# Hybrid pooling / short-convolution decoder layer: the third convolution term on ScalarE and GpSimd, more tile buffers, other load conditions and another order

## The chip, the cores and the metric

The program runs on the 8 cores of one Trainium2 chip, each with a different part of the batch and no exchange between them. The metric is the device time of one execution, that of the slowest core, in microseconds. On every core TensorE (PE in the profile), VectorE (DVE), ScalarE (ACT), GpSimd (POOL) and SyncE (SP) each work through an instruction queue of their own in a fixed order. GpSimd and SyncE also issue the transfers.

## What is computed

Each core takes one prompt of 2048 rows and 16 decode sequences of 4 rows (64 rows), all 1024 wide. The reference, cut:

```
h = rmsnorm(x, g_pre_mix) * (1 + sc1) + sh1          # sc1, sh1, gt1, ... = silu(c) @ w_ada + b_ada
v_pool, x_conv, gate_b, gate_c = split(h @ w_in)     # 512 columns each
y_pool = pool_mixer([pool_buf, v_pool]) * pool_scale # windows 2/4/8/16, one 128x128 map per group
y_conv = gate_b * causal_dwconv([conv_buf, gate_c * x_conv], conv_w)   # 3 taps
x = x + gt1 * rmsnorm([y_pool | y_conv] @ w_out, g_post_mix)
h2 = rmsnorm(x, g_pre_ffn) * (1 + sc2) + sh2
a, b = split(causal_dwconv([ffn_buf, h2 @ ffn_w_up], ffn_conv_w))      # 2 x 2816 columns, 3 taps
x = x + gt2 * rmsnorm((silu(a) * b) @ ffn_w_down, g_post_ffn)
```

A `causal_dwconv` with three taps is `p[t-2]*w0 + p[t-1]*w1 + p[t]*w2`. Also returned are the last rows of the pooling input, the convolution input and the up-projection.

## The kernel before

**Stages.** Rows go in tiles of 128: tiles 0 to 15 are the prompt, tile 16 the 64 decode rows. Columns of the transposed activation `ah` go in chunks of 512 rows of the sequence (c = 0 to 3) and chunk 4 for the decode rows.

1. Start: `tile_in(t)` loads a pair of x tiles, ScalarE squares and sums a tile, a square root and a reciprocal follow, VectorE scales it into `xn` (three buffers, which the square also uses as its junk output), TensorE transposes it (8 matmuls against `idb`) and VectorE or ScalarE copies the result to `ah`. Meanwhile GpSimd issues eight `scp` loads, each with one slice of the scale weights and one of the pooling weights. `scale_in(kc)` turns a slice into the factor `g1t`, `start_step(kc, c)` multiplies `ah` by it and adds slice kc to the pooling projection of chunk c, in banks that seven projections hold together.
2. Projections: `pool_one(g, c)` (`P:`), `pool_win(g, c)` (`W:`, windows on VectorE), `conv_mm(j, c)` (24 matmuls into three banks, weights in `ring` buffers), `conv_mid(j, c)`. For a prompt chunk `conv_mid` does: ScalarE x_conv + bias from a bank into `xc`; VectorE `q` = (gate_c + bias) * `xc` from a second bank; ScalarE gate_b + bias from the third bank into `tb`; ScalarE `ta` = w2 * q; VectorE twice `ta` += w * q for the other taps; GpSimd `by` = `ta` * `tb`. `xc`, `q`, `ta` and `tb` have two buffers each, used in turn. There are 16 such prompt units and 4 small ones (chunk 4, 64 elements).
3. `pool_fold` (`F`) multiplies the pooling map into `wo`, the 4 MB of w_out that `wout_load` (`w`) loads into a region where the pooling inputs `v` lay.
4. Output projection: `o_step` runs tile by tile: 16 matmuls `wo,by`; norm on ScalarE; scaling with the gate row `gtp` on VectorE; four additions of 128x256 on GpSimd to x loaded again; store of y; the next norm, and transposes four steps later. `gtp` comes through a scratch tensor in HBM (`gate_scratch`).
5. FFN: `up_group(0)`, down-projection, `up_group(1)`, down-projection, over `w_up` slices in the three `ring` buffers (`up_load`, first three only after `gtp`).

**What sets the order.** The text `PROJ` gives the steps of stages 1 to 3 in TensorE's order (letters as in the table `steps`: `T` tile_in, `a` scale_in, `s` start_step, `m`/`v` the two halves of a conv unit, `U` a whole one, `A` the second set of scale vectors, `w` the w_out load). A planner, `Sched.order`, then plays the whole program with costs (`c_act`, `c_dve`, `c_pool`, `RATE`) and fixes the order of each engine: an instruction's key is the first TensorE step that needs it. Up to a planned time of 70 us a transfer also waits for the last one that had landed in the plan. `keep_warm` puts matmuls on zeros (`ps<-zero`) where the plan sees TensorE wait over 0.5 us. `Region.alias` makes a buffer wait for the last uses of what lay there before.

## Time and profile before

| | us |
|---|---|
| median of three runs | 727.0 (725.28 to 727.85) |
| the profiled execution, its own time | 726.18 |
| its span on core 2, the slowest | 724.6 |
| the spans of the eight cores | 718.5 to 724.6 |
| TensorE busy, core 2 | 694.0 (96%) |
| VectorE / ScalarE / GpSimd busy | 468.5 / 311.1 / 267.5 |

The profiled execution took 1.6 us more than the span of its slowest core and is 0.8 us below the median. The mean granted TensorE clock was 0.989 to 0.995 on the eight cores. The page's picture in 40 slices of 18 us shows TensorE at 9 tenths or more nearly everywhere from the seventh slice on, and 5, 8, 8, 9, 9, 8 tenths in the first six. Busy time of TensorE includes the matmuls on zeros.

### The profile page before, as it was taken

The numbers are of one execution on the slowest core, as the hardware profiler recorded it, in microseconds if no ns is written. First come the engines' busy times: TensorE is split into PE (matmuls) and PEld (weight loads), VectorE is DVE, ScalarE is ACT, GpSimd is POOL, SyncE is SP. The second block draws the span as 40 slices with busy tenths as digits, with TensorE's granted clock in tenths as the row PEclk, the third lists the DMA queues.
The fourth block names the chain that finished last, engine by engine and source line by source line (L and its number), as shares of the span: only waits on it lengthen the run. The fifth ranks groups of instructions, "written<-read, shape, count | busy, mean of one in ns | idle before, by whom it ended". The sixth has DMA issues, their size and how long they took to land.

```text
span 724.6 us, 12059 instructions; the slowest of 8 cores (718.5 to 724.6 us)
## 1 busy us (share of the span) xinstructions
PE 694.0 (96%) x4049; PEld 331.3 (46%) x4049; DVE 468.5 (65%) x636; ACT 311.1 (43%) x554; POOL 267.5 (37%) x274
## 2 busy tenths in 40 slices
PE   5889989999989999999999999999999999999996
PEld 2445535444445544444444444444444444444442
DVE  2659699754659998777777411138777777758403
ACT  5255544334657764444544211144454544433111
POOL 1102255333858634424444132214333333223220
PEclk8999999999999999999999999999999999999999
DMA  8999877996999667556899964113335433061422
GB/s 249 161 240 181 194 124 131 156 192 169 178 277 275 221 116 124 97 127 100 147 156 155 221 222 137 58 59 59 59 66 95 74 59 59 1 228 68 144 105 72
DMA packets 23532, 100.71 MB, mean 139 GB/s; under 512 B 3184, under 2 KB 3696, under 8 KB 18608
## 3 DMA queue, kind: packets, MB, share of 16 engines
q0 software_dynamic: 9072, 47.71, 39.9%
q1 hardware_dynamic: 14400, 52.23, 22.6%
...
HBM read 127.02 MB, written 20.63 MB: 204 GB/s over the span
## 4 chain that ended last, share of the span: by engine, by line
PE 73%; DMA 14%; issue 4%; DVE 4%; POOL 2%; ACT 2%; DVEq 0%; SPq 0%; POOLq 0%; ACTq 0%
PE ps L520 72%; DMA big<-x 5%; DMA scp<-w_scp 3%; DMA y<-big 2%; POOL big L559 2%; DMA wsh<-w_sh 1%; DMA ring<-w_inc 1%; PE ps L530 1%; DVE big L555 1%; POOL by L559 1%; DVE ta L555 1%; DVE ss L559 0%; DVE q L555 0%; PE ps L538 0%; ACT xc L551 0%
## 5 line engine op out<-in xcount | busy, mean ns | idle before, releaser
L520 PE MATMUL ps<-ah,ring 128*128 128x512 bf16 (+2 forms) x2240 | 407.2, 342 | 4.4 <-DVE q L555 2.0
L520 PEld LDWEIGHTS ps<-ah,ring 128*128 128x128 bf16 x2240 | 187.8, 98 | 212.8 <-issue 6.6
L555 DVE SCALAR_TENSOR_TENSOR big<-ps,misc,big 128x1022 f32<-128x1022 f32 (+1 forms) x176 | 224.5, 1281 | 69.5 <-ACT halob L551 32.5
L559 POOL TENSOR_TENSOR g<-big 128x1024 bf16<-128x1024 f32 x44 | 104.5, 2375 | 171.6 <-DVE big L559 91.0
L551 ACT ACTIVATE big<-ps,misc 128x1024 f32<-128x1024 f32 x88 | 97.9, 1113 | 140.1 <-PE ps L520 139.9
L520 PE MATMUL ps<-wdn,g 128*128 128x512 bf16 x704 | 153.1, 379 | 0.0
L559 POOL TENSOR_TENSOR big<-big 128x256 f32<-128x256 f32 (+2 forms) x51 | 65.1, 1279 | 121.0 <-DVE big L555 94.1
L520 PEld LDWEIGHTS ps<-wdn,g 128*128 128x128 bf16 x704 | 68.5, 98 | 82.1 <-issue 0.4
L551 ACT ACTIVATE big<-ps 128x1024 bf16<-128x1024 f32 (+2 forms) x30 | 28.9, 964 | 123.4 <-PE ps L520 116.2
L666 DVE RECIPROCAL stat<-stat 128x1 f32<-128x1 f32 (+1 forms) x64 | 9.7, 157 | 106.3 <-ACT stat L551 105.6
L520 PE MATMUL ps<-wo,by 128*128 128x512 bf16 x256 | 58.2, 384 | 0.0
L551 ACT ACTIVATE big<-big 128x1024 f32<-128x1024 f32 x44 | 46.5, 1057 | 6.5 <-DVE big L555 4.1
L551 ACT ACTIVATE xn<-big 128x1024 bf16<-128x1024 f32 (+1 forms) x27 | 28.4, 1054 | 43.3 <-PE ps L520 17.6
L520 PEld LDWEIGHTS ps<-wo,by 128*128 128x128 bf16 x256 | 24.9, 99 | 28.3 <-issue 1.3
L555 DVE SCALAR_TENSOR_TENSOR big<-ps,stat,gtp 128x1024 f32<-128x1024 f32 x26 | 33.3, 1280 | 2.3 <-DVE stat L666 1.2
L559 POOL TENSOR_TENSOR by<-ta,tb 128x512 bf16<-128x512 f32 x16 | 25.8, 1613 | 24.0 <-DVE ta L555 21.1
L538 PE MATMUL ps<-idb,xn 128*128 128x128 bf16 (+1 forms) x268 | 21.2, 226 | 11.7 <-DVE xn L564 9.8
L555 DVE SCALAR_TENSOR_TENSOR ta<-q,misc,ta 128x512 f32<-128x512 f32 x32 | 24.6, 778 | 5.3 <-ACT ta L551 4.8
L538 PEld LDWEIGHTS ps<-idb,xn 128*128 128x128 bf16 (+1 forms) x268 | 17.7, 102 | 19.9 <-issue 16.1
L564 DVE TENSOR_SCALAR xn<-big,stat 128x1024 bf16<-128x1024 f32 (+1 forms) x27 | 23.0, 859 | 0.5
L570 POOL DMA_DIRECT2D ring<-w_up x22 | 12.8, 583 | 21.9 <-PE ps L520 21.9
L520 PE MATMUL ps<-ah,scp 128*128 128x512 bf16 (+1 forms) x104 | 18.9, 332 | 1.8 <-ACT tb L551 1.0
...
## 6 DMA issues: line engine op xcount, KB each, us to landing
...
wdn<-w_down POOLq DMA_DIRECT2D x11, 512.0 KB, 12.8
wg<-w_gate POOLq DMA_DIRECT2D x4, 1024.0 KB, 11.1
...
```

The source lines that it names most:

```text
L520: inst = e.matmul(bank_ap, l, r, start=(first and i == 0), stop=(last and i == len(pairs) - 1))
L530: inst = e.matmul(o, ls[i], r, start=(i == 0), stop=(i == len(ls) - 1))
L538: inst = e.transpose(o, i, ident)
L551: return K.op("act", lambda e: e.activation(out=out, in_=in_, func=func, **kw), reads=reads, writes=writes, cost=c_act(n, ptr))
L555: return K.op(eng, lambda e: e.scalar_tensor_tensor(out, in0, s, in1, op0, op1), reads=reads, writes=writes, cost=c_dve(n))
L559: return K.op(eng, lambda e: e.tensor_tensor(out, in0, in1, op), reads=reads, writes=writes, cost=c_dve(n) if eng == "dve" else c_pool(n))
L564: return K.op("dve", lambda e: e.tensor_scalar(out, in0, s1, None, op0), reads=reads, writes=writes, cost=c_dve(n, mode), port=mode > 1.0)
L570: return K.dma(eng, lambda e: [e.dma_start(out=dst, in_=src)], sem or next_misc(), 1, reads=reads, writes=regs, deps=deps, nbytes=nbytes)
L666: K.op("dve", lambda e: e.reciprocal(STAT[0:rows, k + 1, t:t + 1], STAT[0:rows, k + 1, t:t + 1]), reads=[r_stat[k + 1][t]], writes=[r_stat ...
```

## The change

- `conv_mid`: tap w0 is no longer added by VectorE. ScalarE writes w0 * q into `xc` (free once q is made), GpSimd adds it to `ta`, VectorE adds tap w1 with its one remaining multiply-add, and VectorE, not GpSimd, multiplies by `tb`. The same for the 4 small units.
- `pool_win` on chunk 4: the 10 running sums over `vs` go from VectorE to GpSimd. The four scalings of the pooling map (`poolw`) and the four 15-column state copies (`npp`) go from VectorE to ScalarE.
- Norms: tiles 0 to 7 have 7 `xn` buffers in place of 3, and the squares of the first norm write to `junk` buffers. The second norm of the prompt tiles writes to 8 `xnp` buffers, which lie where the w_ss weights were.
- A square root without use runs on ScalarE right after the first activation, so that its table is loaded then.
- `wout_load`: the first half of `wo` waits for `v` of groups 0 and 1 only, the second for `v` of groups 1 (second buffer), 2 and 3; before, both waited for all of `v`, `vs` and `pwf`.
- `PROJ` is another text (all tokens of the start are interleaved: chunk 0 is projected before tiles 5 and 7 are turned), and some planner costs are other numbers (`RATE` 315e3 for 330e3; `c_pool`, `c_dve`).
- `turn_by_dma` and `UPAT` are added but not used: with `FIRST_T = 16` every turn stays on TensorE, and with `UPAT = (-1, -1, -1)` the first `w_up` loads wait for the gate row as before.

```diff
 PROJ = """
-T:0 T:1 T:2 T:3 T:4 T:5 T:6 T:7 a:0 s:0,0 s:0,1 a:1 s:1,0 s:1,1 a:2 s:2,0 s:2,1 a:3 s:3,0 s:3,1 a:4 s:4,0 s:4,1
+T:0 T:4 T:1 a:0 T:2 T:3 T:6 a:1 a:2 s:0,0 T:7 T:5 s:1,0 s:0,1 s:2,0 s:1,1 a:3 s:3,0 s:2,1 s:3,1 a:4 a:5 a:6
...
+FIRST_T = 16
+UPAT = (-1, -1, -1)
...
-    RATE = 330e3
+    RATE = 315e3
...
+    K.op("act", lambda e: e.activation(out=STAT[:, 7, 19:20], in_=EPSB, func=AF.Sqrt), reads=[r_sc, r_eps], cost=0.3)
...
+        if k == ST2 and t < 16:
+            N, r_n = XNP[t % 8], r_xnp[t % 8]
+        else:
+            j = t % (NXN + 4) if t < 8 else t % NXN
+            N, r_n = XN[j], r_xn[j]
...
+        if k == ST1:
+            h = t % 2 if t < 8 else 0
+            stats(X[0:rows, :], rows, k, t, [r_x], JUNK[h][0:rows, :], [r_junk[h]])
...
-            ts(POOLW[:, g, :], PWF[:, g, :], VECS[:, V_PSC + g:V_PSC + g + 1], None, ALU.mult, None, [r_pwf, r_vecs], [r_poolw], 128)
+            act(POOLW[:, g, :], PWF[:, g, :], AF.Copy, [r_pwf, r_vecs], [r_poolw], 128, scale=VECS[:, V_PSC + g:V_PSC + g + 1])
...
-                tt(dst[:, lo:W], src[:, lo:W], src[:, lo - sh:W - sh], ALU.add, [r_src], [r_dst], W - lo)
+                tt(dst[:, lo:W], src[:, lo:W], src[:, lo - sh:W - sh], ALU.add, [r_src], [r_dst], W - lo, eng="pool")
...
         act(sh(TA[k]), v[2], AF.Copy, [rq, r_vecs], [r_ta[k]], n, scale=w2)
-        for m, w in ((1, w1), (0, w0)):
-            stt(sh(TA[k]), v[m], w, sh(TA[k]), ALU.mult, ALU.add, [rq, r_ta[k], r_vecs], [r_ta[k]], n)
+        act(sh(XC[k]), v[0], AF.Copy, [rq, r_vecs], [r_xc[k]], n, scale=w0)
+        tt(TA[k][:, 0:n], TA[k][:, 0:n], XC[k][:, 0:n], ALU.add, [r_ta[k], r_xc[k]], [r_ta[k]], n, eng="pool")
+        stt(sh(TA[k]), v[1], w1, sh(TA[k]), ALU.mult, ALU.add, [rq, r_ta[k], r_vecs], [r_ta[k]], n)
         if c < 4:
-            tt(BY[:, 4 + j, c0:c0 + n], TA[k], TB[k], ALU.mult, [r_ta[k], r_tb[k]], [r_by[4 + j][c]], n, eng="pool")
+            tt(BY[:, 4 + j, c0:c0 + n], TA[k], TB[k], ALU.mult, [r_ta[k], r_tb[k]], [r_by[4 + j][c]], n)
...
-            ts(NPP[:, g, :], VB[g][1][:, 528 - PB:528], BIAS[:, g:g + 1], None, ALU.add, None, [r_v[g][1], r_bias], [r_npp], PB)
+            act(NPP[:, g, :], VB[g][1][:, 528 - PB:528], AF.Identity, [r_v[g][1], r_bias], [r_npp], PB, bias=BIAS[:, g:g + 1])
...
             for r in r_wo[hb]:
-                r.alias(pool_regs)
+                r.alias(r_v[0] + r_v[1] if hb == 0 else r_v[1][1:] + r_v[2] + r_v[3])
```

**How the order moves.** TensorE in the start, before: all eight tiles are turned (`idb,xn`), then the slices `scp_59` to `scp_66` are worked off in pairs.

```order
L538 MATMUL ps<-idb_50,xn_96 128x128 x8
L538 MATMUL ps<-idb_50,xn_97 128x128 x8
L513 MATMUL ps<-zero_127 128x512 x12
L538 MATMUL ps<-idb_50,xn_95 128x128 x8
L538 MATMUL ps<-idb_50,xn_96 128x128 x8
L520 MATMUL ps<-sc_45,scp_59 128x18 x8
L520 MATMUL ps<-sc_45,scp_60 128x18 x8
L810 MATMUL ps<-ah_87,scp_59 128x512 x7
```

The same place now:

```order
L519 MATMUL ps<-zero_139 128x512 x17
L544 MATMUL ps<-idb_50,xn_105 128x128 x8
L544 MATMUL ps<-idb_50,xn_119 128x128 x8
L526 MATMUL ps<-sc_45,scp_60 128x18 x8
L837 MATMUL ps<-ah_95,scp_59 128x512 x4
L837 MATMUL ps<-ah_95,scp_60 128x512 x4
L544 MATMUL ps<-idb_50,xn_122 128x128 x8
L526 MATMUL ps<-sc_45,scp_61 128x18 x8
```

Chunk 0's projections (x4) now stand after five tiles; behind the last slice stand 13 matmuls on zeros ahead of tile 8, where none stood, and 6 more ahead of the first use of the second `ring` weights. In all there are 82 such matmuls for 59.

VectorE, first conv units after the decode rows' bias is known, before (with what each waits for):

```order
L555 SCALAR_TENSOR_TENSOR q_99<-raw_89,bias_52,xc_101 128x512 [waits e_pool]
L555 SCALAR_TENSOR_TENSOR by_88<-s_114,v_123 128x512 [waits e_act]
L555 SCALAR_TENSOR_TENSOR by_88<-s_113,v_121 128x512 [waits e_dve]
L564 TENSOR_SCALAR poolw_125<-pwf_126,misc_43 128x128
L555 SCALAR_TENSOR_TENSOR by_88<-s_112,v_118 128x512
L555 SCALAR_TENSOR_TENSOR ta_103<-q_99,misc_43,ta_103 128x512 [waits e_act]
```

And now:

```order
L561 SCALAR_TENSOR_TENSOR ta_111<-q_107,misc_43,ta_111 128x512 [waits e_pool]
L565 TENSOR_TENSOR by_96<-ta_111,tb_113 128x512 [waits e_dve]
L561 SCALAR_TENSOR_TENSOR ta_112<-q_108,misc_43,ta_112 128x512 [waits e_pool]
L561 SCALAR_TENSOR_TENSOR q_107<-ps,bias_52,xc_109 128x512 [waits e_pool,e_pe,e_act]
L565 TENSOR_TENSOR by_96<-ta_112,tb_114 128x512 [waits e_dve]
L561 SCALAR_TENSOR_TENSOR q_108<-ps,bias_52,xc_110 128x512 [waits e_pe,e_pool,e_act]
```

`ta` and `q` now both stand behind waits for GpSimd, and the `poolw` scalings are gone from here.

GpSimd at the end of the projections, before: the first of the three first `w_up` loads (`ring_78`) waits for the gate row, the other two for matmuls that still use their buffers, `ring_77` for those of the last conv unit.

```order
L559 TENSOR_TENSOR by_88<-ta_103,tb_105 128x512
L570 DMA ring_78<-w_up 128x4096
L570 DMA ring_79<-w_up 128x4096
L570 DMA ring_77<-w_up 128x4096
L1015 COPY qlast_108<-q_100 128x2
L559 TENSOR_TENSOR by_88<-ta_104,tb_106 128x512
```

And now:

```order
L565 TENSOR_TENSOR ta_111<-ta_111,xc_109 128x512
L576 DMA ring_86<-w_up 128x4096
L576 DMA ring_85<-w_up 128x4096
L1046 COPY qlast_116<-q_108 128x2
L576 DMA ring_87<-w_up 128x4096
L565 TENSOR_TENSOR ta_112<-ta_112,xc_110 128x512
```

`ring_85`, which waited for the last conv unit, now waits for an earlier one (unit 3 of chunk 3 comes earlier in `PROJ`) and stands ahead of `ring_87`. The gate row's own matmuls (`wg,sc`) come 7.8 us of TensorE work sooner, and SyncE's store of it stands ahead of one store that it stood behind. On the same queue the two `wo` loads stood behind all six w_ss loads and two products; now they directly follow the fifth w_ss load, ahead of the sixth.

## Rows read from the trace of the kernel before

**Rows 1.** Windows, core 2: start:end, length, busy time by engine, clock, DMA share, GB/s
```profile
core 2: us, PE busy (x) PEld busy (x) DVE busy (x) ACT busy (x) POOL busy (x), PEclk, DMA share, GB/s
14.00:52.00 38.00, 31.29 (x242) 17.00 (x243) 22.95 (x57) 14.65 (x37) 5.12 (x11) 0.94 1.03 212
52.00:82.00 30.00, 30.00 (x271) 16.30 (x269) 23.55 (x54) 17.12 (x40) 5.50 (x6) 1.00 1.00 198
82.00:140.00 58.00, 53.04 (x393) 26.16 (x391) 54.61 (x106) 24.07 (x48) 30.00 (x41) 0.97 0.82 138
140.00:176.00 36.00, 35.17 (x206) 16.42 (x205) 18.05 (x30) 14.92 (x23) 9.97 (x15) 1.00 0.87 174
176.00:242.00 66.00, 62.17 (x366) 31.01 (x365) 46.99 (x81) 44.46 (x95) 49.22 (x63) 0.97 0.95 243
242.00:282.00 40.00, 39.00 (x204) 18.51 (x203) 39.13 (x50) 24.64 (x44) 18.93 (x16) 1.00 0.63 136
```

**Rows 2.** Timeline of TensorE around 105 us: start, us, what, idle before it
```profile
103.12 2.72 PE L520 MATMUL ps<-ah,ring 128*128 128x512 bf16 x8 [1.98 <-DVE q L555]
105.64 2.79 PE L520 MATMUL ps<-ah,scp 128*128 128x512 bf16 x8
108.26 1.89 PE L520 MATMUL ps<-ah,ring 128*128 128x512 bf16 x8
```

**Rows 3.** Start: TensorE at 73 us, the issue of the second ring load, its landing time
```profile
73.42 8.53 PE L520 MATMUL ps<-ah,ring 128*128 128x512 bf16 x80
...
62.53 0.53 POOL L570 DMA_DIRECT2D ring<-w_inc  x1 [1.28 <-DMA wsh<-w_sh]
...
ring<-w_inc POOLq DMA_DIRECT2D x1, 768.0 KB, 11.1
```

**Rows 4.** Instruction groups of VectorE in 78 to 176 us: count, busy us, mean ns
```profile
L555 DVE SCALAR_TENSOR_TENSOR ta<-q,misc,ta 128x512 f32<-128x512 f32 x32 | 24.6, 778 | 5.3 <-ACT ta L551 4.8
L559 DVE TENSOR_TENSOR ss<-ss 128x301 f32<-128x301 f32 (+2 forms) x6 | 3.7, 613 | 0.2
L564 DVE TENSOR_SCALAR poolw<-pwf,misc 128x128 bf16<-128x128 f32 x4 | 3.1, 768 | 0.0
L564 DVE TENSOR_SCALAR npp<-v,bias 128x15 f32<-128x15 f32 x4 | 2.9, 735 | 0.0
L559 DVE TENSOR_TENSOR ss<-vs 128x303 f32<-128x303 f32 x4 | 1.9, 470 | 0.0
L559 DVE TENSOR_TENSOR s<-v 128x512 f32<-128x512 f32 x1 | 0.7, 710 | 0.8 <-ACT v L551 0.8
```

**Rows 5.** The same groups of ScalarE and GpSimd
```profile
L551 ACT ACTIVATE ta<-q,misc 128x512 f32<-128x512 f32 x16 | 11.5, 721 | 14.9 <-DVE q L555 13.0 <-DVE s2t L564 1.9
...
L559 POOL TENSOR_TENSOR by<-ta,tb 128x512 bf16<-128x512 f32 x15 | 24.5, 1634 | 24.0 <-DVE ta L555 21.1 <-DVE by L555 1.9 <-ACT tb L551 0.8
```

**Rows 6.** Timeline of VectorE: the same eight scalings without and with GpSimd at work
```profile
58.96 2.17 DVE L564 TENSOR_SCALAR ah<-ah,g1t 128x512 bf16<-128x512 bf16 x8
...
85.86 3.20 DVE L564 TENSOR_SCALAR ah<-ah,g1t 128x512 bf16<-128x512 bf16 x8
```

**Rows 7.** Output projection: GpSimd's timeline, two steps of the chain, TensorE's timeline
```profile
176.78 1.66 POOL L570 DMA_DIRECT2D ring<-w_up  x3 [5.72 <-PE ps L520]
...
183.73 15.74 DMA y<-big
...
199.58 10.81 DMA big<-x
...
217.29 1.01 PE L538 MATMUL ps<-idb,xn 128*128 128x128 bf16 x8 [3.34 <-DVE xn L564]
218.09 4.61 PE L520 MATMUL ps<-wo,by 128*128 128x512 bf16 x16
```

**Rows 8.** SyncE: a wait for the gate row's store, and the issue of its load
```profile
SPq L301 <- DMA gate_scratch<-big: 18.8, 1, 18.8
...
166.71 0.80 SPq L1126 DMA_DIRECT2D gtp<-gate_scratch  x2
```

More of the change, by code:

```diff
@@ L396, in build_program @@
     W2 = [alloc("w2", [128, 2, KC, 128], BF16, at=cur[0] + 4096 * i) for i in range(4)]
+    XNP = [alloc("xnp", [128, D], BF16, at=cur[0] + 2048 * i) for i in range(8)]
     USB = alloc("usb", [128, NPAIR, 2, NS, 6], F32)
@@ L429, in build_program @@
     SS = [alloc("ss", [128, NS * (PB + DS)], F32) for _ in range(2)]
+    XN += [alloc("xn", [128, D], BF16, at=cur[0] + 2048 * i) for i in range(4)]
     SB_ = [alloc("s", [128, 512], F32) for _ in range(4)]
@@ L677, in stats2 @@
              writes=[r_stat[k + 1][16]], cost=0.16)
-    r_xn = [R() for _ in range(NXN)]
-    xn_i = [0]
+    r_xn = [R() for _ in range(NXN + 4)]
+    r_junk = [R() for _ in range(2)]
     r_ah = [[R() for _ in range(17)] for _ in range(KC)]
@@ new lines, in norm_tile, with turn_by_dma @@
+        if k == ST1:
+            h = t % 2 if t < 8 else 0
+            stats(X[0:rows, :], rows, k, t, [r_x], JUNK[h][0:rows, :], [r_junk[h]])
+        else:
+            stats(X[0:rows, :], rows, k, t, [r_x], N[0:rows, :], [r_n])
+        ts(N[0:rows, :], X[0:rows, :], STAT[0:rows, k + 1, t:t + 1], None, ALU.mult, None,
+           [r_x, r_stat[k + 1][t]], [r_n], D, mode=2.0)
+        return N, r_n
+    r_xnp = [R() for _ in range(8)]
+    s_xnp = [new_sem("xnp%d" % i) for i in range(8)]
+    def turn_by_dma(t):
+        K.dma("sp", lambda e: [e.dma_start_transpose(out=AH[:, :, t * 128:t * 128 + 128], in_=XNP[t - 8])], s_xnp[t - 8], 1,
+              reads=[r_xnp[t - 8]], writes=[r_ah[kc][t] for kc in range(KC)], deps=[up_op[-1]], nbytes=524288, row=2048)
+        if t % 4 == 3:
+            modulate(list(range(t - 3, t + 1)), G2T, S2T, r_m2)
@@ L701, in turn_tile @@
+    def turn_tile(t, xn, eng, bank=None):
         r0, rows = tile_rows(t)
+        N, r_n = xn
         b = take() if bank is None else bank
         psb = PSF[:, b, :].bitcast(BF16).rearrange("p (k n) -> p k n", k=KC)
[L704 to L705 removed]
+        o = tr([psb[:, kc, 0:rows] for kc in range(KC)], [N[0:rows, kc * 128:(kc + 1) * 128] for kc in range(KC)],
+           IDB[0:rows, 0:rows], [r_n, r_idb], [r_bank[b]], 0.5)
@@ L819, in tile_in @@
         turn_tile(t, p1a[t], TURNS[t], (turn_b + [None])[t % (5 - START)] if t < 8 else None)
+        if t == 7:
+            r_ta[0].alias(r_junk[1:])
+            for i in range(4):
+                r_s[i].alias(r_xn[NXN + i:NXN + i + 1])
     def start_step(kc, c):
```

62 lines of the change are left out of this document (30 added, 32 removed).

## The prediction

> **What bounds the kernel now.** I read the windows of the trace first [rows 1], then TensorE's timeline and waits, then the other engines where TensorE waits. The useful matmuls are the same ones before and after; only TensorE's idle and slow time can go. In the windows the reader is to compare TensorE's busy time with the window's length: 52 to 82 us is full (30.00 of 30), 82 to 140 lacks 4.96 us, 140 to 176 lacks 0.83, 176 to 242 lacks 3.83, 242 to 282 lacks 1.00 [rows 1]. From there to the last few microseconds TensorE is full too, and the change touches nothing there. So the change can earn only in four places:
>
> - 14 to 52 us: 6.71 us idle, and more in matmuls on zeros. The DMA share is 1.03, and 1.00 in the next window [rows 1]: transfers set this stretch.
> - 82 to 140 us: 4.96 us idle, and a slower clock after the longest wait. Granted clock 0.97 over the window; two groups of eight matmuls took 2.72 and 2.79 us where the next one at the upper level took 1.89 [rows 2], which is 0.83 + 0.90 = 1.73 us. Sum 6.7 us. VectorE is busy 54.61 of 58 us here [rows 1]: its `q` is what TensorE's banks wait for longest, 1.98 us [rows 2].
> - 140 to 176 us: 0.83 us, at the fold, which needs w_out.
> - 176 to 242 us: 3.83 us, nearly all one hole of 3.34 us at 217, after which the turns took 1.01 and the projection 4.61 us, where 16 matmuls of 0.216 and their latency are 3.6: 1.0 us more [rows 7]. Sum 4.8 us (the 0.4 of the turns left out). The chain behind it: a y store took 15.74 us, the x load into its buffer 10.81, then GpSimd's addition, the norm, the turn. The three w_up loads, 2 MB of HBM reads each, were issued at 176.78, just ahead of that store [rows 7]. They had waited for the gate row, whose own load was issued at 166.71 after 18.8 us of waiting for its store [rows 8].
>
> **The start.** Tiles are turned sooner, chunk 0 is projected while tiles 5 to 7 still arrive, and table and buffers are ready. But the second `ring` load is issued at 62.53 and lands 11.1 us later, at 73.6; the matmuls that use it start 1.7 us into the group of 73.42, at 75.1 [rows 3]. Ahead of that first use TensorE now has 41.1 us of useful work since the first turn instead of 42.8 (I added the orders up: 0.216 us per 512-column matmul, 1.89 us per eight with its latency [rows 2]). One group of eight, 1.7 us, went behind it. So the new start can be ready at 73.4 and must wait to 73.6: the same point within 0.3 us, and the tiles 14 and 15 follow after equal work. This fits the zeros put there (13 ahead of tile 8, 6 ahead of this load). The transfers are not shorter, only the first `scp` slice is issued sooner, and the queue was full. I take **0**; bounds -2 (if transfers gain from the earlier first issue) to +1 (23 more matmuls on zeros at 0.216 are 5.0 us; they stand before waits for transfers, and cost only where those come early).
>
> **The conv stretch, 82 to 140 us.** What leaves VectorE: 16 of 32 additions `ta` of 0.778 (12.4 us), against 16 products of 0.71 that arrive (11.4); the ten sums (3.7 + 1.9 = 5.6), `poolw` 3.1 and `npp` 2.9 [rows 4]. Net 1.0 + 5.6 + 3.1 + 2.9 = 12.6 us, nearly all of it from a stretch in which VectorE had 3.4 us to spare [rows 1]. What arrives: on ScalarE 16 scalings of 0.72 [rows 5], 11.5 us and some 2 us of small ones, against 34 us idle there; on GpSimd the product of 1.63 is exchanged for an addition of the same shape, and ten sums of 300 elements come, at 300/512 of 1.63 about 1.0 each, so 10 us on top of 30.00 busy of 58 [rows 1, 5]. All these fit.
>
> What is new is latency. A unit's chain was ta, two additions, product; it is now ta, scaling, GpSimd's addition, one multiply-add, product: + 0.72 + 0.71 - 0.78 = 0.65 us, and one handover more, some 0.15 us as an estimate between the neighbouring rows. And `xc` stays taken until GpSimd has added, so the evacuation of the bank of x_conv two units later waits for GpSimd. With 24 matmuls or 5.2 us of TensorE work a unit, a chain of about 7 us with two buffers per name has room on average, not when several units are due at once (at 80 to 100 us). I take **-4.0** of the 6.7; bounds -6.7 and +6 (half of the units exposed, below).
>
> The Trainium skill, page "SBUF — State Buffer", section "Who interferes with whom", says that VectorE's second SBUF input comes through a port shared with GpSimd, that copies, casts and scalings in a fast mode take the whole shared pair, and that the one who comes second is fully blocked. The trace agrees for the scalings: eight took 2.17 us with GpSimd idle, 3.20 with it at work [rows 6]; for the multiply-adds with two SBUF inputs it hardly shows on VectorE's side (0.778 mean against 0.710 for another two-input one [rows 4]). By the rule at its strictest, each of the 26 added or moved GpSimd sums would hold a VectorE instruction for about half its time, 26 x 0.7 = 18 us, more than the 12.6; the term would then be 0.
>
> **The fold.** w_out no longer waits for the store of the pooling state and for all of `v`; it is issued right behind five w_ss loads rather than after six and two products. I take **-0.8**, bounds -0.8 and +1 (the order of TensorE around it is tight again).
>
> **The output projection.** The gate row's matmuls come 7.8 us of TensorE work sooner, and w_ss and w_out, which its store queues behind, are free to start when the last `scp` matmul is done, 5.2 us of work sooner. So the gate row should be there, and two w_up loads issued, some 10 us earlier, into a stretch whose DMA share was 0.87 (140 to 176) [rows 1], and 4 of 6 MB need not compete with the first y stores. If the store that took 15.74 takes 8 to 10 and the load behind it 9, the hole of 3.34 is gone: GpSimd's addition would come 6 to 8 us sooner. The eight `xnp` buffers also take away the wait of a norm for the turn of three tiles before; the trace shows no loss there, so nothing for it. What is late next is VectorE, 46.99 of 66 here and 39.13 of 40 in the next window [rows 1]; the latter stretch is partly work put off by the hole. I take **-4.0** of 4.8; bounds -4.8 and 0. The 1.00 us of 242 to 282 I leave as it is (-1 to +1).
>
> **Sum.** 0 - 4.0 - 0.8 - 4.0 = -8.8. Against the profiled execution's 726.18: 717.4; the median of the runs lies 0.8 higher, so 718.2.
>
> **Rivals.**
>
> A, only the transfers' part comes: in the conv stretch the shared port or the longer chain takes back what VectorE's relief gives. For it: VectorE's order now has `ta` and `q` behind waits for GpSimd, and GpSimd's queue holds transfer issues that wait for TensorE. Against: GpSimd is busy 30.00 of 58. Without the -4.0: 722.2. Chance 0.16, with 721.5 to 724.8.
>
> B, the start earns as well. For it: 14 to 52 us has 6.71 us idle. Against: the DMA share is full to 82. If the second ring load lands 3.5 us sooner, 714.7; with all of the conv stretch too (-2.7 more) 712. Chance 0.10, from 711 to 714.5.
>
> C, nothing that counts: the store of the gate row reaches HBM as late as before, w_up stays where it was, the hole stays, and in the conv stretch one wait replaces another. 726.2 to 727.5. Chance 0.11.
>
> D, slower: GpSimd is now inside each unit's chain, and TensorE waits for it. The place is the bank of x_conv, held until `xc` is free, behind GpSimd's addition and whatever load issue stands before it. Price 0.8 us a unit (0.65 + 0.15), 12.8 us if all 16 are exposed and none of the 6.7 returns; with the 4.8 of fold and output kept, 727.0 + 12.8 - 4.8 = 735.0. It decides from 6 exposed units of 16 on (4.8 / 0.8); at half of the units 728.6. Against: on the mean a unit has 5.2 us of TensorE work to hide in. Chance 0.11.
>
> **How the numbers follow.** The forecast case, 714.5 to 721.5, has 0.52. About 0.3% is what a measurement of this kernel can tell from no change, so faster means below 724.8: 0.52 + 0.16 + 0.10 = 0.78; same 0.11 (C); slower 0.11 (D). The range for 8 in 10 leaves out D and the lower part of B: 713 to 727.
>
> **What would show it.** Right: windows of 82 to about 135 with TensorE idle under 3 us and no clock loss; VectorE some 11 us less busy over the projections; the ring load's landing still near 73.6 and the first w_up issue before 170; no wait over 1 us of TensorE for `xn` in the output projection, y stores under 10 us. Wrong: TensorE or ScalarE's `xc` waiting for GpSimd's `ta` by several us (A, D); the first w_up issue again 3 us after the last projection (C); TensorE at tiles 14 and 15 before 79 us (B).

## The result and the profile after

The changed kernel took 729.5 us (median of 17 runs, 727.2 to 730.5), the kernel before 726.4 (17 runs, 722.8 to 728.4) on the same chip: ratio 1.0042, 95% interval 1.0030 to 1.0054. It is 0.4% slower where 8.8 us less were forecast. Some executions, of any kernel here, run with one die at a lower clock and take over 1.5% longer; they are left out of every time, ratio and mean below. The profiled execution's slowest core is core 7 with a span of 728.9 us. Its windows, to be read against [rows 1]:

```profile
core 7: us, PE busy (x) PEld busy (x) DVE busy (x) ACT busy (x) POOL busy (x), PEclk, DMA share, GB/s
14.00:52.00 38.00, 34.95 (x258) 17.56 (x257) 24.64 (x60) 17.19 (x41) 5.02 (x11) 0.97 1.01 217
52.00:82.00 30.00, 28.30 (x257) 14.92 (x255) 21.89 (x48) 13.82 (x33) 3.94 (x6) 1.00 1.02 203
82.00:140.00 58.00, 52.08 (x367) 24.87 (x368) 46.67 (x77) 32.38 (x65) 36.04 (x50) 0.94 0.82 147
140.00:176.00 36.00, 36.00 (x211) 16.95 (x209) 18.76 (x36) 19.67 (x34) 13.36 (x24) 1.00 0.89 174
176.00:242.00 66.00, 64.35 (x396) 32.09 (x395) 51.27 (x84) 45.13 (x96) 47.14 (x59) 1.00 0.89 240
242.00:282.00 40.00, 36.78 (x184) 17.00 (x183) 35.52 (x48) 26.29 (x44) 16.34 (x16) 0.96 0.54 116
```

VectorE was relieved as planned (46.67 of 58 us where it had 54.61), and TensorE lacks more there than before (5.92 us, and a clock of 0.94; the other seven cores have 0.97 or 1.00). The last window lacks 3.22 us where it lacked 1.00. The slowest cores are different ones, so I read the same five marks on all eight cores from their timelines: the arrival of tile 14's rows, the first matmul of the output projection (`wo`), of the up projection, of the second gate row (`wg`), and the end. Means of eight cores, one execution of each kernel, us:

| | data 14 | to `wo` | `wo` to up | up to `wg` | `wg` to end | span |
|---|---|---|---|---|---|---|
| before | 77.90 | 94.80 | 66.08 | 58.73 | 424.09 | 721.60 |
| after | 77.41 | 95.26 | 65.79 | 62.02 | 424.57 | 725.05 |
| a_silu | 76.37 | 95.27 | 65.97 | 59.01 | 424.51 | 721.14 |
| b_silu | 77.58 | 94.94 | 64.53 | 63.66 | 424.02 | 724.73 |
| b_conv | 77.95 | 97.24 | 69.00 | 59.40 | 424.16 | 727.75 |
| b_conv_dve | 77.77 | 94.15 | 66.58 | 59.01 | 424.22 | 721.73 |
| b_wout | 78.13 | 96.29 | 62.93 | 61.95 | 424.28 | 723.58 |
| b_lite | 77.82 | 93.09 | 68.52 | 59.20 | 424.30 | 722.93 |
| a_oldboth | 77.41 | 94.63 | 64.45 | 58.49 | 424.46 | 719.44 |
| ob_nostart | 77.75 | 98.41 | 64.94 | 58.16 | 424.66 | 723.91 |
| ob_lite | 77.85 | 92.94 | 64.08 | 61.68 | 424.72 | 721.27 |
| b_k2 | 78.18 | 97.11 | 65.07 | 58.52 | 424.60 | 723.48 |
| ob_k | 77.88 | 94.29 | 67.18 | 59.60 | 424.02 | 722.98 |

From one execution of a kernel to the next the mean span of its eight cores scatters (standard deviation 0.2 to 1.0 us over the runs of each kernel; 0.8 for the kernel before), so differences of a few tenths in this table say nothing, and b_k2's row is of the quickest of its twelve executions (their mean is 725.0).

From before to after one stretch grew on every core: up to `wg`, 58.68 to 58.80 us on all eight before, 61.14 to 62.82 after. The stretches in which I had forecast -4.8 and -4.0 moved by +0.46 and -0.29 on the mean.

**Where the 3.3 us are.** TensorE in the changed kernel, core 7:

```profile
252.03 5.34 PE L526 MATMUL ps<-ah,ring 128*128 128x512 bf16 x24
259.84 0.61 PE L544 MATMUL ps<-idb,xnp 128*128 128x128 bf16 x8 [2.46 <-DVE xnp L570]
260.28 0.39 PE L544 MATMUL ps<-idb,xn 128*128 128x128 bf16 x4
261.13 43.29 PE L526 MATMUL ps<-ah,ring 128*128 128x512 bf16 x192 [0.46 <-ACT big L557]
```

ScalarE on the same core (`ACT_TABLE_LOAD` brings in the table of another function; the row with `xnp<-big` is the squares of tile 15, `big<-big` the Silu of the first up half, `stat<-stat,eps` the root of tile 15):

```profile
252.83 1.05 ACT L557 ACTIVATE xnp<-big 128x1024 bf16<-128x1024 f32 x1
...
254.20 1.28 ACT L557 ACT_TABLE_LOAD   x1
255.50 1.06 ACT L557 ACTIVATE big<-big 128x1024 f32<-128x1024 f32 x1
256.57 1.28 ACT L557 ACT_TABLE_LOAD   x1
257.87 0.29 ACT L557 ACTIVATE stat<-stat,eps 128x1 f32<-128x1 f32 x1
...
264.42 1.28 ACT L557 ACT_TABLE_LOAD   x1 [2.17 <-DVE big L561]
```

The root of tile 15 could have run at 254.2. The planner put the Silu ahead of it, so ScalarE loads Silu's table, runs it, loads the root's table back, and only then is the norm of tile 15 made; TensorE stands for it 2.46 us (2.46 or 2.47 on all eight cores). And the 192 matmuls behind take 43.29 us, where the kernel before has 3.61 + 13.97 + 24.33 = 41.9 for as many. The clock in the windows around:

```profile
252.00:257.00 5.00, 5.00 (x28) 2.29 (x25) 3.61 (x6) 4.95 (x8) 0.00 (x0) 1.00 0.27 107
257.00:260.00 3.00, 0.54 (x5) 0.19 (x4) 1.73 (x4) 2.65 (x6) 0.57 (x1) 1.00 0.03 3
260.00:263.00 3.00, 2.54 (x18) 1.27 (x16) 3.00 (x3) 2.25 (x3) 1.71 (x1) 0.79 1.00 167
263.00:266.00 3.00, 3.00 (x10) 1.15 (x9) 3.00 (x5) 1.57 (x2) 1.19 (x2) 0.65 0.97 188
```

A granted clock of 0.65 is a mixture of the levels of 1.2 and 2.4 GHz, after an idle TensorE.

### The profile page after: what moved, and what is told of

Read it like the earlier page. It is cut to its first block, busy times and chain, and to the rows that moved or that the text cites. A ratio compares the mean times of both kernels' runs of the same rounds, so it can differ in the third digit from the quotient of the medians.

```text
span 728.9 us, 12128 instructions; the slowest of 8 cores (722.9 to 728.9 us)
## 1 busy us (share of the span) xinstructions
PE 701.2 (96%) x4072; PEld 332.2 (46%) x4072; DVE 464.1 (64%) x614; ACT 327.0 (45%) x585; POOL 273.1 (37%) x288
## 4 chain that ended last, share of the span: by engine, by line
PE 73%; DMA 12%; DVE 4%; issue 4%; POOL 3%; ACT 2%; DVEq 0%; SPq 0%; POOLq 0%; ACTq 0%
PE ps L526 71%; DMA big<-x 4%; DMA y<-big 2%; DMA scp<-w_scp 2%; DMA ring<-w_inc 2%; POOL big L565 1%; PE ps L536 1%; DMA bigp<-x 1%; DMA big<-xs 1%; DMA wsh<-w_sh 1%; ACT big L557 1%; DVE s L946 1%; DVE big L561 1%; DVE ta L561 1%; DVE xnp L570 0%
## 5 line engine op out<-in xcount | busy, mean ns | idle before, releaser
L561 DVE SCALAR_TENSOR_TENSOR big<-ps,misc,big 128x1023 f32<-128x1023 f32 (+1 forms) x176 | 224.4, 1281 | 74.3 <-ACT halob L557 34.9
L557 ACT ACTIVATE junk<-big 128x1024 bf16<-128x1024 f32 (+1 forms) x15 | 15.7, 1049 | 34.1 <-DMA big<-x 32.7
L565 POOL TENSOR_TENSOR ta<-ta,xc 128x512 f32<-128x512 f32 (+1 forms) x20 | 23.3, 1170 | 16.9 <-ACT xc L557 9.5
L519 PE MATMUL ps<-zero 128*128 128x512 bf16 x82 | 21.8, 415 | 1.9 <-DVE zero L587 1.9
L572 DVE TENSOR_SCALAR ah<-ah,g2t,s2t 128x512 bf16<-128x512 bf16 x32 | 21.0, 686 | 1.1 <-ACT ah L557 1.1
L557 ACT ACTIVATE ta<-q,misc 128x512 f32<-128x512 f32 x16 | 11.5, 718 | 18.2 <-DVE q L561 18.2
L561 DVE SCALAR_TENSOR_TENSOR ta<-q,misc,ta 128x512 f32<-128x512 f32 x16 | 14.7, 921 | 7.5 <-POOL ta L565 7.5
```

The source lines that it names most:

```text
L519: o.pad = lambda e: e.matmul(ap, ZERO[:, 0:ap.shape[0]], ZERO[:, 0:n], start=first, stop=first)
L557: return K.op("act", lambda e: e.activation(out=out, in_=in_, func=func, **kw), reads=reads, writes=writes, cost=c_act(n, ptr))
L561: return K.op(eng, lambda e: e.scalar_tensor_tensor(out, in0, s, in1, op0, op1), reads=reads, writes=writes, cost=c_dve(n))
L565: return K.op(eng, lambda e: e.tensor_tensor(out, in0, in1, op), reads=reads, writes=writes, cost=c_dve(n) if eng == "dve" else c_pool(n))
L572: return K.op("dve", lambda e: e.tensor_scalar(out, in0, s1, s2, op0, op1), reads=reads, writes=writes, cost=c_dve(n, mode), port=mode > 1.0)
```

## Experiments

Times are ratios to the kernel before on the same chip, with 95% intervals; 1% is 7.3 us. The runs were made in five sessions on three chips, so a comparison of two of them from different sessions (the `ob_` runs and a_best against a_oldboth) goes by way of the kernel before.

One reading serves all of them. The time is that of the slowest core, and the slowest core lies 3.9 to 4.4 us over the mean of the eight in the kernel before, but only 1.8 to 2.3 us in b_wout, a_oldproj, a_oldboth, a_best, ob_nostart and ob_noxnp. A kernel can so gain time while its mean core gains none.

### The two function tables: a_silu and b_silu

a_silu is the changed kernel with the first half's Silus kept behind the last root:

```diff
-        act(STAT[0:rows, k + 1, t:t + 1], ..., AF.Sqrt, ...)
+        roots.append(act(STAT[0:rows, k + 1, t:t + 1], ..., AF.Sqrt, ...))
...
-            act(BIG[ma], BIG[ma], AF.Silu, [r_big[ma]], [r_big[ma]], 1024)
+            silu = act(BIG[ma], BIG[ma], AF.Silu, [r_big[ma]], [r_big[ma]], 1024)
+            if gi == 0:
+                silu.deps.add(roots[-1])
```

> The changed kernel with one added dependency: in the first half of the up projection no Silu of ScalarE is ordered ahead of the last square root of the norms behind the output projection. All else is the changed kernel. Theory T (function tables): the new order put the first Silu of the up projection between tile 15's squares and its root, so ScalarE loads a table, runs Silu 1.06 us, and loads the old table back (two loads of 1.28 us more than before, a third Silu-ward load later); the turn of tile 15 waits 2.46 us on TensorE and the matmuls behind run slowly for a few us. In the two traces the time from the first up matmul to the first wg matmul is 58.7 us on all eight cores before and 61.1 to 62.8 after. With the root ahead of the Silu this stretch should fall to 58.7 to 59.2 on all cores and the kernel to 725.5 to 727, 3 to 4 us below the changed kernel and within 0.3% of the one before. Rival L (the chain of tile 15 is late by itself, or the slow clock comes from elsewhere): the stretch stays at 61 to 63 and the time at 729.

0.9989 (0.9970 to 1.0007), 0.53% or 3.8 us under the changed kernel, each by its ratio to the kernel before. ScalarE and TensorE now (core 2):

```profile
250.94 0.30 ACT L557 ACTIVATE stat<-stat,eps 128x1 f32<-128x1 f32 x1
...
252.32 1.28 ACT L557 ACT_TABLE_LOAD   x1
...
254.13 0.61 PE L544 MATMUL ps<-idb,xnp 128*128 128x128 bf16 x8
```

One load, no wait for tile 15, and 59.0 us from up to `wg` on every core. b_silu puts the detour into the kernel before:

```diff
+        if k == ST2 and t == 15:
+            extra = [K.op("act", lambda e: e.activation(out=STAT[:, 7, 19:20], in_=EPSB, func=AF.Silu),
+                          reads=[r_eps, r_stat[k][t]], cost=0.3)]
...
+        root.deps.update(extra)
```

> The kernel before with one more instruction: a Silu on one column, its result unused, between tile 15's squares and its square root behind the output projection, which the root waits for. All else is the kernel before. Theory T (function tables): the detour through the Silu table costs here what it costs in the changed kernel: two table loads of 1.28 us more, the stretch from the first up matmul to the first wg matmul grows from 58.7 to 61 to 63 us on all cores, and the time from 726.4 to 729 to 730. Rival L (it is hidden, the loss of the changed kernel came from elsewhere in its new order): within 0.5 us of the kernel before.

1.0054 (1.0032 to 1.0077), 3.9 us slower; up to `wg` 63.0 to 64.3 us on all cores:

```profile
251.64 1.28 ACT L666 ACT_TABLE_LOAD   x1
...
254.22 1.28 ACT L551 ACT_TABLE_LOAD   x1
...
258.28 1.01 PE L538 MATMUL ps<-idb,xn 128*128 128x128 bf16 x8 [3.48 <-ACT big L551]
```

In a_silu only ScalarE's order differs from the changed kernel's, and only in that the Silu stands three instructions later; in b_silu every engine's order is that of the kernel before up to the same place (behind it a few instructions are moved too). So theory T is shown from both sides: the switch costs 3.8 and 3.9 us of time, 3.0 and 4.9 us in this stretch of the mean core (in b_silu the granted clock behind the wait is 0.50 for 6 us). The Trainium skill, page "ScalarE: Activation LUTs", section "Rules for kernel authors", says to budget about 2.7 us for every switch of set; its section "What ACT_TABLE_LOAD costs" adds that up from some 1283 ns a load and some 1380 ns of a drain. Each load is 1.28 us here. By the 2.7 an estimate for the two switches ahead of the root would be 5.4 us on ScalarE; the rows show 2.56 and no time for a drain, since each load starts within 0.02 us of the end of the instruction ahead of it.

### The middle of the conv units: a_oldconv, b_conv, b_conv_dve

a_oldconv is a_silu with this edit reversed, b_conv is the kernel before with this edit alone:

```diff
-        for m, w in ((1, w1), (0, w0)):
-            stt(sh(TA[k]), v[m], w, sh(TA[k]), ...)
+        act(sh(XC[k]), v[0], AF.Copy, [rq, r_vecs], [r_xc[k]], n, scale=w0)
+        tt(TA[k][:, 0:n], TA[k][:, 0:n], XC[k][:, 0:n], ALU.add, ..., eng="pool")
+        stt(sh(TA[k]), v[1], w1, sh(TA[k]), ...)
...
-            tt(BY[:, 4 + j, c0:c0 + n], TA[k], TB[k], ALU.mult, ..., eng="pool")
+            tt(BY[:, 4 + j, c0:c0 + n], TA[k], TB[k], ALU.mult, ...)
```

> The changed kernel with the table repair of a_silu, and with the old middle of the conv units: both multiply-adds on VectorE, the product on GpSimd, no second scaling on ScalarE. If the new middle earns the 4 us that the prediction gave it, this is 4 us slower than a_silu, some 730. If the relief of VectorE is eaten by the longer chain and the shared port (rival A), it is within 1 us of a_silu. If the longer chain costs more than the relief brings (rival D), it is 1 to 4 us faster than a_silu. From the per-core traces (fold of w_out reached 0.5 us sooner on the mean of eight cores) I expect the second: within 1 us.

0.9957 (0.9939 to 0.9976), 0.32% or 2.3 us faster than a_silu; the two intervals just overlap, but the mean core says the same (718.9 us for 721.5). Its trace is not read here, only its time.

> The kernel before with one part of the change alone: the new middle of the conv units (third term scaled on ScalarE into xc, added on GpSimd, product on VectorE). The prediction's step put the relief of VectorE at a gain; alone it would leave VectorE 1.0 us less and the chain of a unit 0.8 us longer. Theory G, from a_oldconv against a_silu (0.32% faster without it): this is 1.5 to 3.5 us slower than the kernel before, 728 to 730. If the prediction's relief held: 722 to 726.

1.0081 (1.0061 to 1.0101): 5.9 us slower by the ratio, 7.1 by the medians. TensorE, ScalarE, GpSimd and VectorE of core 0:

```profile
102.12 2.27 PE L520 MATMUL ps<-ah,ring 128*128 128x512 bf16 x5 [4.98 <-ACT xc L551]
...
99.19 0.22 ACT L551 ACTIVATE xc<-ps 128x64 f32<-128x64 f32 x1 [1.80 <-POOL ta L559]
101.05 0.35 ACT L551 ACTIVATE xc<-qs,misc 128x64 f32<-128x64 f32 x1 [1.63 <-DVE qs L559]
101.30 0.67 ACT L551 ACTIVATE xc<-ps,bias 128x512 f32<-128x512 f32 x1
...
96.82 3.44 POOL L559 TENSOR_TENSOR ta<-ta,xc 128x512 f32<-128x512 f32 x2 [1.23 <-ACT xc L551]
...
99.16 1.66 DVE L555 SCALAR_TENSOR_TENSOR ta<-q,misc,ta 128x512 f32<-128x512 f32 x1 [1.17 <-POOL ta L559]
```

This is the place that rival D named: a bank waits for `xc`, `xc` for GpSimd's addition, and VectorE stands in the same line. b_conv_dve moves only the addition to VectorE and the product back:

```diff
-        tt(TA[k][:, 0:n], TA[k][:, 0:n], XC[k][:, 0:n], ALU.add, ..., eng="pool")
+        tt(TA[k][:, 0:n], TA[k][:, 0:n], XC[k][:, 0:n], ALU.add, ...)
...
-            tt(BY[:, 4 + j, c0:c0 + n], TA[k], TB[k], ALU.mult, ...)
+            tt(BY[:, 4 + j, c0:c0 + n], TA[k], TB[k], ALU.mult, ..., eng="pool")
```

> b_conv with its addition on VectorE in place of GpSimd and the product back on GpSimd: VectorE's load is that of the kernel before (an addition for a multiply-add), a unit's chain is longer by ScalarE's scaling of 0.72 us, and xc is held until VectorE has added. b_conv measured 1.0081 of the kernel before. Theory G (GpSimd's addition inside the chain is what costs: TensorE stood 4 to 5 us for xc, ScalarE for GpSimd's ta): within 1 us of the kernel before. If the scaling and the held xc cost by themselves: 730 or more.

0.9994 (0.9976 to 1.0013). The longer chain and the held `xc` alone cost nothing that can be measured; with GpSimd in it they do, as far as two kernels can tell whose orders differ too. The wait for `xc` is there in b_conv on all eight cores, 3.99 to 4.98 us at one conv unit. But the stretch up to `wo` grew by only 2.4 us on the mean core, since the kernel before has waits there too (0.99 and 1.98 us at 100 and 103 us on core 2). 2.9 us more came in the output projection, where the hole of [rows 7] is now on all eight cores (1.5 to 6.3 us). Whether the later arrival there or the new order made it is not separated (see b_k2).

### The sums on GpSimd: a_oldss, a_oldconv_ss, a_best, b_ss

```diff
-                tt(dst[:, lo:W], src[:, lo:W], src[:, lo - sh:W - sh], ALU.add, ..., W - lo, eng="pool")
+                tt(dst[:, lo:W], src[:, lo:W], src[:, lo - sh:W - sh], ALU.add, ..., W - lo)
```

The reason to try it were VectorE's and GpSimd's rows in the changed kernel: a window sum (`s<-v,s`) took 1.27 us with no addition of GpSimd beside it and 1.71 with one, and VectorE stood 1.79 us for a sum of GpSimd's that lay behind eight issues of weight loads.

```profile
116.59 1.71 DVE L946 TENSOR_TENSOR_SCAN s<-v,s 128x512 f32<-128x512 f32 x1
...
120.94 1.27 DVE L946 TENSOR_TENSOR_SCAN s<-v,s 128x512 f32<-128x512 f32 x1
...
125.67 1.32 DVE L561 SCALAR_TENSOR_TENSOR by<-ss,vs 128x64 bf16<-128x64 f32 x1 [1.79 <-POOL ss L565]
...
117.36 2.50 POOL L565 TENSOR_TENSOR ss<-ss 128x301 f32<-128x301 f32 x2
119.82 2.69 POOL L576 DMA_DIRECT2D w<-w_ss  x5
122.46 0.57 POOL L576 DMA_DIRECT2D wo<-w_out  x1
123.56 0.53 POOL L576 DMA_DIRECT2D wo<-w_out  x1 [0.53 <-DVE by L561]
124.08 0.55 POOL L576 DMA_DIRECT2D w<-w_ss  x1
...
124.74 0.82 POOL L565 TENSOR_TENSOR ss<-ss 128x289 f32<-128x289 f32 x1
```

> The changed kernel with the table repair of a_silu, and with the ten running sums of the samples (ss) back on VectorE; the new middle of the conv units stays. Theory G (GpSimd in VectorE's line): in the changed kernel's trace VectorE stands 1.79 us at 124 us for a sum on GpSimd that lies behind seven issues of weight loads, and two scans and an addition just before the q that TensorE waits 1.97 us for took 0.4 us more each while GpSimd added. So this earns 0.5 to 2 us against a_silu. Rival V (VectorE's relief counts): the 5.6 us of sums return to a full engine and it is 1 to 3 us slower than a_silu.

0.9968 (0.9945 to 0.9990), 0.2% under a_silu, which the intervals don't separate. Its mean core is 1.9 us under that of the kernel before, where a_silu's is 0.3 over; the slowest core doesn't follow.

> The changed kernel with the table repair of a_silu, and with both of what the change gave GpSimd between VectorE's steps taken back: the old middle of the conv units and the sums ss on VectorE. a_oldconv (sums still on GpSimd) measured 0.9957 of the kernel before and a_silu 0.9989. Theory G: the sums cost something there too, so 0.993 to 0.9957. Rival V: VectorE becomes the bound as in the kernel before, and it is slower than a_oldconv: 0.9957 to 1.000.

0.9947 (0.9931 to 0.9962), beside 0.9957 of a_oldconv: not separated either.

> As a_oldboth (table repair, old middle of the conv units, old order), and the ten sums ss back on VectorE too. So of the change it keeps: the start's buffers and early table, poolw and npp on ScalarE, the aliases of w_out, the eight xnp buffers. a_oldboth measured 0.9926 of the kernel before. Theory G (anything of GpSimd in VectorE's line costs): 0.990 to 0.9926. If the sums were only harmful beside the new middle (a_oldconv_ss against a_oldconv: 0.1% and inside its interval): 0.992 to 0.994.

a_best is a_oldboth (next section) with the same edit: 0.9976 (0.9963 to 0.9989), 0.5% slower than a_oldboth (0.4% by the medians). Theory G falls as a rule.

> The kernel before with the ten sums ss on GpSimd alone, and the first Silu kept behind the last two roots. a_best against a_oldboth says that they earn 0.5% on GpSimd, a_oldss against a_silu that they cost 0.2% there. If relief counts and GpSimd has room when it is not in the units' chain: 1 to 3.5 us faster than the kernel before. If the sums in GpSimd's queue hold VectorE: 0.5 to 2 us slower.

1.0018 (0.9999 to 1.0036) for the reverse edit in the kernel before (with the roots kept ahead of the Silu): neither.

### The written order: a_oldproj and a_oldboth

```diff
-T:0 T:4 T:1 a:0 T:2 T:3 T:6 a:1 a:2 s:0,0 T:7 T:5 s:1,0 s:0,1 s:2,0 s:1,1 a:3 s:3,0 s:2,1 s:3,1 a:4 a:5 a:6
...
+T:0 T:1 T:2 T:3 T:4 T:5 T:6 T:7 a:0 s:0,0 s:0,1 a:1 s:1,0 s:1,1 a:2 s:2,0 s:2,1 a:3 s:3,0 s:3,1 a:4 s:4,0 s:4,1
...
```

> The changed kernel with the table repair of a_silu, and with the old written order of the projections (start, conv units, gate row, fold as in the kernel before); new engines, own buffers and the w_out aliases stay. If the order carries the gain of the change, this is 2 to 5 us slower than a_silu. If it carries none, within 1 us. If the new order (tiles in another sequence, v:1,4 late) costs time that the engines' relief had gained, it is faster than a_silu by 1 to 3 us. I expect 1 to 3 us slower.

0.9973 (0.9955 to 0.9991): the old order is 0.16% better than the new one, inside the intervals, and not 1 to 3 us worse.

> The changed kernel with the table repair, the old middle of the conv units and the old written order of the projections; sums on GpSimd, poolw and npp on ScalarE, buffers and aliases of w_out as changed. a_oldconv measured 0.9957 and a_oldproj 0.9973 of the kernel before, a_silu 0.9989. If the two parts are independent this is 0.994 (722.2). If the new order was made for the new middle and helps with it alone, 0.993; if the old order brings back the old hole of the output projection on some cores, 0.997 to 1.000.

Old order and old middle of the units: 0.9926 (0.9909 to 0.9943), 722.9 us in six executions. This beats both kernels, the one before by 5.4 us by the ratio and 4.6 by the medians; 2.6 of that are in the mean core, the rest in a slowest core that lies nearer to it.

### Single parts in the kernel before: b_wout, b_lite

Both keep the roots ahead of the first Silu; each has one part of the change:

```diff
# b_wout
-                r.alias(pool_regs)
+                r.alias(r_v[0] + r_v[1] if hb == 0 else r_v[1][1:] + r_v[2] + r_v[3])
# b_lite
-            ts(POOLW[:, g, :], PWF[:, g, :], VECS[:, V_PSC + g:V_PSC + g + 1], ...)
+            act(POOLW[:, g, :], PWF[:, g, :], AF.Copy, ..., 128, scale=VECS[:, V_PSC + g:V_PSC + g + 1])
...
-            ts(NPP[:, g, :], VB[g][1][:, 528 - PB:528], BIAS[:, g:g + 1], ...)
+            act(NPP[:, g, :], VB[g][1][:, 528 - PB:528], AF.Identity, ..., bias=BIAS[:, g:g + 1])
```

> The kernel before with the aliases of w_out of the change alone (it waits for v of its own stretch of memory, not for all of v, the pooling state and its store), and with the order of the first Silu behind the last two roots kept. The prediction gave the earlier w_out 0.8 us at the fold and, through the earlier gate row and w_up loads, up to 4 us in the output projection. If the prediction's term holds it is 1 to 4.8 us faster (722 to 725.5). If the hole of the output projection is not set by when w_up is issued (it was on three of eight cores before, and on none in b_silu, with the same issue times of 171 to 178 us): within 1.5 us of the kernel before.

1.0010 (0.9994 to 1.0025). The table shows why: the output projection takes 62.7 to 63.4 us on the eight cores (66.1 on the mean before) and the hole is gone, as forecast (b_silu, without this edit, has no hole either, and 64.5 us); 3.2 us come back in the next stretch (61.95 for 58.73), and 1.5 in the stretch ahead. The mean core is 2.1 us slower and the slowest core the same. Part of the 3.2 are waits for VectorE: 2.6 us on core 2, where the kernel before has 1.0. TensorE's waits in 236 to 300 us on core 2:

```profile
PE ps L520 <- DVE big L555: 2.6, 3, 1.4
PE ps L538 <- ACT halo L551: 0.5, 1, 0.5
PE ps L538 <- DVE xn L564: 0.3, 1, 0.3
```

> The kernel before with poolw and npp on ScalarE alone, eight instructions and 6.0 us less on VectorE in the conv stretch and no handover added to any chain; the first Silu is kept behind the last two roots. If VectorE's relief by itself pays (the prediction's reason for the conv stretch, without the GpSimd step): 2 to 4 us faster. If not: within 1 us.

1.0017 (1.0000 to 1.0033): 6.0 us less on VectorE in its fullest stretch earn nothing in time. The table has more: up to `wo` b_lite is 1.7 us shorter than the kernel before (92.9 to 93.7 us on the eight cores, 94.1 to 95.4 there), and it loses 2.4 us in the output projection, where six cores have a hole of 2.0 to 7.1 us. Whether the 1.7 us are the relief is not shown: ob_lite below puts the same work back on VectorE and is 1.7 us shorter there too.

### One part taken out of the best kernel: ob_nostart, ob_noxnp, ob_lite

```diff
# ob_nostart: three xn buffers for tiles 0 to 7, squares into xn, no early root
-            j = t % (NXN + 4) if t < 8 else t % NXN
+            j = t % NXN
# ob_noxnp: the second norms write to the xn buffers
-        if k == ST2 and t < 16:
-            N, r_n = XNP[t % 8], r_xnp[t % 8]
# ob_lite: the reverse of b_lite
```

> a_oldboth (0.9926 of the kernel before) without the parts of the start: tiles 0 to 7 use the three xn buffers again, squares write to xn, no early square root. The prediction gave the start 0. In the traces the first turn comes at 12.6 us in every kernel with these parts and at 13.9 without (means of eight cores). If the start is set by the transfers up to the second ring load, this is within 0.5 us of a_oldboth (0.992 to 0.9935). If the 1.3 us of the first turn are carried through: 0.994 to 0.995.

1.0011 (0.9997 to 1.0025), 0.85% slower than a_oldboth. But tile 14's rows arrive at 77.75 (77.41 there): the start's own effect is 0.3 us. The loss is in the stretch behind, 98.41 for 94.63, where of this edit only the squares of the last tiles lie, right at its start and with another buffer to write to.

> a_oldboth without the eight xnp buffers: the second norms write to the three xn buffers again. The prediction gave them nothing. From before to a_oldboth the output projection's stretch fell from 66.1 to 64.5 us on the mean of eight cores. If the own buffers did that, this is 1 to 3 us slower than a_oldboth (0.994 to 0.997); if it was the earlier w_up loads, within 0.5 us of it.

0.9941 (0.9919 to 0.9963): not separated from 0.9926.

> a_oldboth with poolw and npp back on VectorE (6.0 us more there, 5 us less on ScalarE). In the kernel before, moving them to ScalarE alone measured 1.0017: nothing or a small loss. If VectorE's relief pays once the rest is in place: 1 to 3 us slower than a_oldboth (0.994 to 0.997). If it does nothing: 0.992 to 0.9935.

0.9995 (0.9976 to 1.0014), 0.7% slower, where the same move alone in the kernel before was worth nothing. The loss is not where the work went: up to `wo` the mean core is 1.7 us faster than a_oldboth's, and from up to `wg` it is 3.2 us slower (60.4 to 63.1 us on the eight cores, 58.4 to 58.6 there). TensorE and VectorE there on core 4:

```profile
264.45 7.07 PE L526 MATMUL ps<-ah,ring 128*128 128x512 bf16 x32 [0.90 <-DVE big L561]
273.79 26.02 PE L526 MATMUL ps<-ah,ring 128*128 128x512 bf16 x112 [2.26 <-DVE big L561]
...
258.38 3.12 DVE L572 TENSOR_SCALAR ah<-ah,g2t,s2t 128x512 bf16<-128x512 bf16 x3
```

VectorE's order in this stretch is another one than in a_oldboth, where the longest of these waits is 0.24 us on this core.

### The order alone: b_k2 and ob_k

Edits seemed to cost where they aren't. These two change no useful work, engine or buffer, only the planner's constants. With them the planner draws another order (94 of VectorE's 638 instructions are moved in b_k2) and places its matmuls on zeros anew (71 for 59 in b_k2, 70 for 79 in ob_k); b_k2 is the kernel before with the new ones, ob_k is a_oldboth with the old ones (both with the roots kept ahead of the first Silu, as the kernel before has them anyway):

```diff
-    RATE = 330e3
+    RATE = 315e3
...
-        return (0.16 if mode > 1.0 or n < 256 else 0.21) + n / 960.0 / mode
+        return (0.19 if n < 256 else 0.16 if mode > 1.0 else 0.21) + n / 960.0 / mode
...
-        return 0.15 + n * 2.2 / 1000.0
+        return 0.15 + n * (2.2 if n < 512 else 2.7) / 1000.0
```

> The kernel before with the changed planner constants alone (transfer rate 315 in place of 330 thousand, costs of short VectorE and long GpSimd operations), and the first Silu kept behind the last two roots. No work, engine or buffer changes, only the order in which the planner puts it. Theory O (order drawn anew): the time from tile 14's data to the output projection (94.8 us before on the mean of eight cores) and the one from there to the first wg matmul (124.8) shift by 1 to 4 us each, one way or the other, and the time by 0.2 to 0.6%. Rival W (the differences between the neighbours were the work's): within 0.15% of the kernel before.

1.0039 (1.0020 to 1.0059).

> a_oldboth (0.9926 of the kernel before) with the old planner constants. Theory O: somewhere from 0.991 to 0.999, mostly slower, since a_oldboth is the best draw of the ones measured. Rival W: 0.992 to 0.9935.

1.0014 (0.9998 to 1.0031), 0.9% slower than a_oldboth. b_k2 has more matmuls on zeros and ob_k fewer, and both are slower, so their number doesn't explain it. So what the planner draws, by itself, moves this kernel by 0.4 to 0.9%, as much as any part of the change, and every edit above but those of a_silu and b_silu draws it anew over much of the program. The single differences of 0.2 to 0.8% among the neighbours above can't be put down to the work that was moved; only the table switch (order elsewhere unchanged) and the wait seen in b_conv's rows can.

Where the draw loses can partly be read. Of the 3.5 us of ob_k's mean core 2.7 are in the output projection, where four cores have the hole of [rows 7] again and a_oldboth has none:

```profile
214.96 0.61 PE L544 MATMUL ps<-idb,xnp 128*128 128x128 bf16 x8 [4.55 <-ACT stat L557]
```

It is the same place as in the kernel before (3.34 us on core 2), b_conv and b_lite. b_k2's loss is up to `wo` instead (97.11 for 94.80).

## Why the prediction was wrong

- **242 to 282 us, "I leave as it is": +3.3 us on the mean core, 3.8 in the time.** The step that failed worst. The written order of ScalarE had changed here (Silu before the last root), and I had read orders only where I expected gains. Neither the cost of a table load nor its place stood in my sum; the runs showed two loads of 1.28 us and a Silu ahead of a root that TensorE waits for (a_silu takes them away, b_silu puts them into the kernel before). The change of order itself was there to be read.
- **Conv stretch, -4.0: nothing came.** From tile 14's data to `wo` 94.80 became 95.26. VectorE's relief came about (7.9 us less in 82 to 140), but TensorE there waits for single steps, not for VectorE's total: the waits at 103 and 124 us for `q` are 1.22 and 1.97 in the changed kernel, behind window sums or behind GpSimd. "All these fit" compared busy sums; GpSimd's part was a handover in an ordered line, behind up to eight weight-load issues. On core 7, the slowest, a low clock follows the wait at 124 us:

```profile
124.00:127.00 3.00, 3.00 (x31) 1.31 (x27) 1.33 (x2) 1.68 (x3) 2.89 (x6) 0.70 1.10 156
127.00:130.00 3.00, 2.22 (x11) 0.85 (x12) 2.78 (x8) 1.44 (x3) 0.96 (x2) 0.50 0.99 130
```

  and its stretch up to `wo` is 96.8 us, where the other seven have 95.0 to 95.3. b_lite has relief without GpSimd in a chain, and it earned nothing in time either; whether it earned the 1.7 us up to `wo` is open.
- **The shared port.** I wrote that on VectorE's side it hardly shows. VectorE's group in 78 to 176 us of the changed kernel, against [rows 4]:

```profile
L561 DVE SCALAR_TENSOR_TENSOR ta<-q,misc,ta 128x512 f32<-128x512 f32 x15 | 14.0, 932 | 7.5 <-POOL ta L565 7.5
```

  932 ns on the mean for 778, and 7.5 us of standing for GpSimd's `ta`. My alternative of 0 for this term was the nearer one.
- **Fold, -0.8:** inside the +0.46 of that stretch, so not seen.
- **Output projection, -4.0: -0.3 on the mean.** The mechanism held: first w_up issue 172.04 (166 to 172 in after and a_silu, 173 to 178 before), the store `y` a median of 7.8 us for 15.1 (five stores up to 215 us), no wait of 3 us. It came 5.6 us earlier on the mean core, not some 10. The price was wrong in two ways. The hole of [rows 7] was on three of eight cores (4.23, 3.34 and 2.24 us on cores 1, 2 and 4), and in b_silu, with the same order there, on none. Core 7, without a hole, ended at 723.9 us, so closing core 2's hole could earn 0.7 us at once, not 4. And what b_wout wins there is lost ahead of it and behind it, in part to VectorE: I named VectorE as next in line and charged 0.
- **Start, 0: right.** Tile 14's data came at 77.90 and 77.41 us; the first turn is 1.2 us sooner (13.85 and 12.68) and it is lost in the transfers.
- **Not in the sum at all:** that all steps keep their order. The rest, 0.5 us from `wg` to the end (424.09 and 424.57), also comes with the order: b_k2 has 424.60 without any other edit, ob_k 424.02 with the old constants.
- **Rivals.** D's place was right (b_conv), its size in the changed kernel small: ScalarE's `xc` waited 1.4 us for GpSimd. Its price of 0.8 us for each of up to 16 units has the wrong form: b_conv has one wait of 4 to 5 us at one unit. C's and A's reasons hold for the terms that didn't come; the loss came from none of the four.

What stays open: why the conv stretch earned nothing (the rows show waits, no experiment took them away with the order kept), and why the best order is the best. Which of its waits a better order could still close was not tried.
